# A hybrid decoder step on one core: old-state products split, residuals fused, z projected during GLA

## The chip, the cores and the metric

The kernel runs on one core of a Trainium2 chip. The metric is the time on the device, in microseconds. Engines are TensorE (PE, its weight loads PEld), VectorE (DVE), ScalarE (ACT), GpSimd (POOL) and SyncE (SP), which issues the transfers.

## The reference, cut to what matters

One layer: RMSNorm, a parallel mixer of gated DeltaNet (8 heads of 128) and GLA (4 heads, 128 by 256), a merge, then a mixture of 32 experts. There are 304 tokens: 272 of a prompt, taken in chunks, and 8 sequences of 4 tokens that begin from given old states.

```
p = h @ w_in                      # q, k, v | z | b, a | q_b, k_b, v_b, r_b | lr | g_a, g_b
# gated DeltaNet, a chunk: M = I + beta * (k k^T) * decay, strictly lower
value, kcd = solve(M, [beta*v, beta*exp(G)*k])
v_new = value - kcd @ S
o_a   = (q*exp(G)) @ S + (q k^T * decay) @ v_new
S     = S*exp(GL) + (k*exp(GL-G))^T @ v_new
# GLA, a chunk: o_b = (q*exp(B)) @ S + A @ v ;  S = S*exp(BL) + (k*exp(BL-B))^T @ v
o_a = rmsnorm(o_a, norm_a) * silu(z)
o_b = rmsnorm(o_b, norm_b) * silu(r_b)
merged = sigmoid(g_a) * (o_a @ w_proj_a) + sigmoid(g_b) * (o_b @ w_proj_b)
x = x + merged @ w_out ;  x = x + experts(rmsnorm(x)) ;  y = rmsnorm(x)
```

## The kernel before

Five functions run one behind the other with a barrier between them: `front` (qkv projection, convolution, norms), `delta` (DeltaNet), `gla`, `merge` (the other projections, gates, output projection), `experts`. Each has one hand-written program per engine; an engine works in the order written, and semaphores are the only links.

**Weights.** A load `n` brings 1 MB (256 columns of `w_in`, or a quarter of a projection) into one of eight ring slots (`load_w`, L223; the slot from `slot(n)`, L69) as soon as PE has used the slot's last content (`unit_done`). ACT makes a rounded high part (`high_part`, L246), DVE or POOL the low part (`low_part`, L252), and PE multiplies a block of 128 columns as 24 matmuls of 304 columns, three for each of 8 slices (`block_of_slot`, L261): two blocks to a load. Loads 20 to 23 are z (N_Z is 20), 24 to 27 are r, 28 to 35 the gates, 36 to 43 the two projections, 44 to 47 `w_out`. Blocks of merge are counted from z: 0 to 7 are z, 8 to 15 r, 16 to 31 the gates, 32 to 47 the projections.

**delta.** PE first does the tail's products (the last 48 tokens: 16 of the prompt, 32 of the samples), then eight q and k projections for GLA with the tail's solve between them (L1202 to L1248), then `old_products` of both halves (L1194, 64 instructions for each 4 heads: the old states, 128 by 128, times 8 columns of keys and queries), then two chunks of 128 tokens. A chunk works on two halves of four heads, `hh`, with a solve whose three last rounds (`for r in range(3)`, L1318) alternate between PE, DVE and ACT; then residual, new values, output and state (L1338 to L1360). In chunk 1 the residual is two DVE operations on 512 columns (L1132, L1133), the state update two more (L1140, L1141), and the same holds for the tail (L1153, L1154, L1173, L1174). POOL prepares gates, masked keys (L975) and decays the old states (L924). DVE copies the old-state products out in 16 pieces (L1092), and POOL's gates of the second half wait for both halves of them (L935).

**gla.** After gate products (L1617, L1618) and decays (L1625, L1627), twelve steps `i`, one per chunk and head: `exps(i + 2)`, ACT's exponents, POOL's scaled keys (L1468), DVE's scaled queries (L1585), `pairs` (L1653), mask and sum on DVE (L1597, L1598), output and state. The last four heads carry the sample states, loaded by SP at the start of the stage (L1442).

**merge.** Twelve norms with blocks 0 to 3 in between (L1867 to L1879), then blocks 4 to 47 (L1880); a block's PSUM bank is free when the block four before it has been read, for z and r by ACT's silu (L1793). DVE gates with it (L1832), ACT and POOL split the gated heads into high and low parts (L1798, L1772). Then comes `w_out`, and the experts start on the result.

## Time and profile before

| | |
|---|---|
| median of 3 runs | 1051.42 us (1048.2 to 1053.07) |
| the profiled execution | 1056.28 us, span 1054.6, mean granted clock 0.873 |
| PE busy in the span | 916.8 us, 87% |
| DVE, ACT, POOL busy | 400.2, 294.3, 282.2 us |
| transfers | 175.67 MB, mean 167 GB/s |

The stages, by the first PE instruction of each: delta from 183.8 us, gla from 410.3, merge from 531.7, the expert stage from about 752. A granted clock of 1.00 is 2.4 GHz and 0.50 is 1.2 GHz. An operation's line is its place in the kernel before; a helper's line (L250, L256, L270 to L272) stands for all its callers. A row of a timeline is start, length, engine, line, operation and, in brackets, the idle time before it and what ended it.

### The profile page before, as it was taken

The numbers are of one execution on the slowest core, as the hardware profiler recorded it, in microseconds if no ns is written. First come the engines' busy times: TensorE is split into PE (matmuls) and PEld (weight loads), VectorE is DVE, ScalarE is ACT, GpSimd is POOL, SyncE is SP. The second block draws the span as 40 slices with busy tenths as digits, with TensorE's granted clock in tenths as the row PEclk, the third lists the DMA queues.
The fourth block names the chain that finished last, engine by engine and source line by source line (L and its number), as shares of the span: only waits on it lengthen the run. The fifth ranks groups of instructions, "written<-read, shape, count | busy, mean of one in ns | idle before, by whom it ended". The sixth has DMA issues, their size and how long they took to land. (4 is left out here: it accounts for less than half of the span.)

```text
span 1054.6 us, 15090 instructions
## 1 busy us (share of the span) xinstructions
PE 916.8 (87%) x6318; PEld 752.7 (71%) x6318; DVE 400.2 (38%) x701; ACT 294.3 (28%) x579; POOL 282.2 (27%) x209
## 2 busy tenths in 40 slices
PE   4989989999989698669988999999669998998963
PEld 3989978998989695446568999999556444444521
DVE  4367833302445432352456531662340222210213
ACT  5453466211222213220056443331201111110102
POOL 7544323313675211133154103755000000000000
PEclk8889999896999755798878999999856999999996
DMA  9624400230000026301485544410471999999981
GB/s 266 202 83 153 153 13 13 83 80 1 2 1 1 1 80 215 125 1 60 140 245 169 160 160 159 160 41 1 170 329 61 421 420 420 420 420 419 419 352 48
DMA packets 97908, 175.67 MB, mean 167 GB/s; under 512 B 8965, under 2 KB 84325, under 8 KB 85494
## 3 DMA queue, kind: packets, MB, share of 16 engines
q1 hardware_dynamic: 97832, 174.62, 45.9%
q8 instruction: 54, 0.88, 0.4%
q14 instruction: 22, 0.17, 0.1%
HBM read 163.66 MB, written 10.95 MB: 166 GB/s over the span
## 5 line engine op out<-in xcount | busy, mean ns | idle before, releaser
L270 PE MATMUL ps<-rounded,rounded 128*128 128x304 f32 x640 | 202.7, 317 | 7.6 <-POOL rounded L256 3.5
L272 PE MATMUL ps<-rounded,rounded 128*128 128x304 f32 x640 | 198.5, 310 | 0.0
L271 PE MATMUL ps<-hL,rounded 128*128 128x304 f32 x512 | 160.4, 313 | 0.0
L256 POOL TENSOR_TENSOR rounded<-ring,rounded 128x2048 fp32r<-128x2048 f32 x24 | 111.1, 4630 | 179.7 <-ACT rounded L250 173.9
L270 PEld LDWEIGHTS ps<-rounded,rounded 128*128 128x128 f32 x640 | 126.1, 197 | 9.4 <-POOL rounded L256 3.7
L272 PEld LDWEIGHTS ps<-rounded,rounded 128*128 128x128 f32 x640 | 125.9, 197 | 0.0
L271 PEld LDWEIGHTS ps<-hL,rounded 128*128 128x128 f32 x512 | 102.1, 199 | 0.4 <-issue 0.2
L250 ACT ACTIVATE rounded<-ring 128x2048 fp32r<-128x2048 f32 x47 | 89.6, 1911 | 27.1 <-PE ps L272 16.0
L2172 DVE TENSOR_TENSOR arena<-arena,ps 128x512 f32<-128x512 f32 (+1 forms) x48 | 32.9, 685 | 123.2 <-PE ps L2290 123.2
L2220 PE MATMUL ps<-arena 128*128 128x128 f32 (+1 forms) x384 | 74.7, 328 | 2.5 <-DVE arena L2139 2.5
L2220 PEld LDWEIGHTS ps<-arena 128*128 128x128 f32 (+1 forms) x384 | 57.1, 204 | 21.6 <-issue 6.2
L2237 PE MATMUL ps<-ring,arena 128*32 128x256 f32 x1024 | 63.2, 404 | 10.2 <-DMA ring<-in_expert_w_up 10.2
L256 DVE TENSOR_TENSOR rounded<-ring,rounded 128x2048 fp32r<-128x2048 f32 x24 | 56.2, 2341 | 36.2 <-ACT rounded L250 36.0
L2237 PEld LDWEIGHTS ps<-ring,arena 128*32 128x32 f32 x1024 | 35.6, 116 | 34.4 <-issue 17.5
L1259 PE MATMUL ps<-arena 128*128 128x128 f32 x448 | 57.1, 288 | 1.1 <-DVE arena L1106 1.1
L1259 PEld LDWEIGHTS ps<-arena 128*128 128x128 f32 x448 | 55.0, 202 | 2.3 <-DVE arena L1106 1.6
L2290 PE MATMUL ps<-arena 128*128 128x512 f32 (+1 forms) x96 | 45.7, 610 | 6.5 <-ACT arena L2062 6.5
L2290 PEld LDWEIGHTS ps<-arena 128*128 128x128 f32 (+1 forms) x96 | 12.9, 166 | 39.5 <-DVE arena L2172 22.0
L2277 PE MATMUL ps<-arena 128*32 128x512 f32 x256 | 31.9, 642 | 9.1 <-DMA arena<-in_expert_w_down 5.0
L2040 ACT ACTIVATE arena<-ps 128x512 f32<-128x512 f32 x16 | 9.6, 597 | 108.5 <-PE ps L2220 108.5
L271 PE MATMUL ps<-rounded,rounded 128*128 128x304 f32 x128 | 38.6, 301 | 0.0
L676 DVE SCALAR_TENSOR_TENSOR arena<-ps,small,arena 128x271 f32<-128x271 f32 (+2 forms) x72 | 35.9, 499 | 2.5
(383 smaller groups left out, 1542.1 us busy)
## 6 DMA issues: line engine op xcount, KB each, us to landing
ring<-in_w_in SPq DMA_DIRECT2D x36, 1024.0 KB, 7.0
ring<-in_expert_w_gate SPq DMA_DIRECT2D x32, 1024.0 KB, 14.4
ring<-in_expert_w_up SPq DMA_DIRECT2D x32, 1024.0 KB, 19.4
arena<-in_expert_w_down SPq DMA_DIRECT2D x32, 1024.0 KB, 17.8
arena<-in_state_gla SPq DMA_DIRECT2D x4, 1024.0 KB, 5.5
out_sg_s<-arena SPq DMA_DIRECT2D x4, 1024.0 KB, 4.1
ring<-in_w_proj_a SPq DMA_DIRECT2D x4, 1024.0 KB, 5.2
ring<-in_w_proj_b SPq DMA_DIRECT2D x4, 1024.0 KB, 5.1
```

Source lines behind the costliest of these rows:

```text
L250: self.nc.scalar.activation(HI[n % 3], self.ring[:, slot(n), :], ACT.Copy).then_inc(self.w_hi, 1)
L256: on.tensor_tensor(self.LOW[:, slot(n), :], self.ring[:, slot(n), :], HI[n % 3], ALU.subtract).then_inc(self.w_lo, 1)
L270: self.nc.tensor.matmul(self.psum[b][:, 0:NT], h[:, j, c], xh(j), start=(j == 0), stop=False)
L271: self.nc.tensor.matmul(self.psum[b][:, 0:NT], h[:, j, c], xl(j), start=False, stop=False)
L272: ins = self.nc.tensor.matmul(self.psum[b][:, 0:NT], lo[:, j, c], xh(j), start=False, stop=(j == KB - 1))
L676: ins = nc.vector.scalar_tensor_tensor(o[:, r:], x[:, 0:TP - r], cw[:, 3 - r, b:b + 1], o[:, r:], ALU.mult, ALU.add)
L1259: ins = mm(bank4(b)[:, h, :], lhs[:, h, :], rhs[:, h, :], start=True, stop=True)
L2172: V.tensor_tensor(y, y, psum[6 + x % 2][0:L[c], :], ALU.add).then_inc(s["y_added"], 1)
L2220: ins = mm(bank4(6 + h)[:, j, :], XN[0:l, c, 128 * b:128 * b + 128], P[0:l, c, :], start=(c == 0), stop=(c == 2))
L2237: ins = mm(psum[kind][32 * i:32 * i + 32, 0:256], XG[:, j, 32 * i:32 * i + 32], w[:, j, :], start=(j == 0), stop=(j == KB - 1))
L2277: ins = mm(psum[4 + half][32 * i:32 * i + 32, :], HX[:, j, 32 * i:32 * i + 32], w[:, j, 512 * half:512 * half + 512], start=(j == 0), stop ...
L2290: mm(psum[6 + x % 2][0:L[c], :], PT[:, T0[c]:T0[c] + L[c]], OG[:, 512 * half:512 * half + 512], start=True, stop=True).then_inc(s["sc_done ...
```

## The change

1. **delta, order.** The first projection block stands ahead of the tail's products; each later one moves up by one place. ACT's evacuations follow.
2. **delta, old-state products.** The first half stays ahead of chunk 0. The second half, into bank 0, stands between rounds 1 and 2 of chunk 0, on keys that POOL has copied aside (`KQ1`). DVE copies each half in two pieces instead of eight; POOL's gates wait for the first half alone.
3. **delta, residuals.** Multiplication and addition are one `scalar_tensor_tensor` for each head, in chunk 1's residual and state and in the tail's.
4. **z in gla.** Loads 20 and 21 go to slots 2 and 3 during delta, 22 and 23 to slots 0 and 1 at the start of gla. The eight z blocks stand in gla: 0 behind the gate products, 1 ahead of `exps(0)`, 2 behind it, 3 to 7 in steps 0 to 4. ACT copies them into `ZR`. Two high parts lie where the sample states go, so those are loaded after the last z block. `exps` of the first two chunks share banks 0 and 1, since the blocks take 4 and 5.
5. **merge.** Blocks 8 to 11 (r) stand between the norms, and PE goes on with 12; the silus of z read `ZR` and wait for no block. Loads of the final norm and the router wait for the eighth gating. The remaining buffers are laid out anew.

```diff
-    return (n if n < N_Z else n + 4) % SLOTS
+    return (n + 6) % 8 % 4 if N_Z <= n < N_Z + 4 else n % SLOTS
...
-        if n >= 3:
-            act.wait_ge(self.unit_done, units(n - 2))
...
+        for n in range(N_Z, N_Z + 2):
+            k.load_w(sp, n)
...
+        V_.tensor_copy(KQ1[:, :, :, :], KQ[:, 4:8, :, TAIL:]).then_inc(s["keys_copied"], 1)
...
-                pl.wait_ge(s["ksq_done"], 2)
-                pl.wait_ge(s["keys_copied"], 2)
+                pl.wait_ge(s["ksq_done"], 1)
+                pl.wait_ge(s["keys_copied"], 3)
...
+        block_out(0)
...
-        block_out(0)
+        block_out(1)
...
+        def old_products_kept(hh, b):
+
+            dve.wait_ge(s["ksq_done"], hh + 1)
+            dve.wait_ge(s["keys_copied"], 3)
+            both = psum[b][:, 0:256].rearrange("p (h b n r) -> p h b n r", h=4, b=8, n=2)
+            for n, dst in enumerate((KT, oaT)):
+                ins = nc.vector.tensor_copy(dst[:, 4 * hh:4 * hh + 4, T0[2] + TAIL:NT].rearrange("p h (b r) -> p h b r", r=TS), both[:, :, :, n, :])
+            ins.then_inc(s["ksq_ready"], 1)
+        old_products_kept(0, 4)
...
+                if c == 0 and r == 1:
+                    old_products_kept(1, 0)
...
                     dve.wait_ge(s["ks_done"], hh + 1)
-                    link(nc.vector.tensor_tensor(w[bB], bank4(b0), bc_last(nbeg[:, c, hs], 128), ALU.mult))
-                    nc.vector.tensor_tensor(w[bB], w[bB], V[:, c, hs, :], ALU.add).then_inc(s["r_ready"], 1)
+                    for h in range(4):
+                        ins = nc.vector.scalar_tensor_tensor(w[bB][:, h, :], bank4(b0)[:, h, :], nbeg[:, c, 4 * hh + h:4 * hh + h + 1], V[:, c, 4 * hh + h, :],
+                                                             ALU.mult, ALU.add)
+                    ins.then_inc(s["r_ready"], 1)
                 dve.wait_ge(s["vn_done"], i + 1)
...
-            link(nc.vector.tensor_tensor(S[:, hs, :], S[:, hs, :], bc_last(egl3[:, 0, hs], 128), ALU.mult))
-            nc.vector.tensor_tensor(S[:, hs, :], S[:, hs, :], bank4(4 * hh + 2), ALU.add).then_inc(s["s_ready"], 1)
+            for h in range(4):
+                ins = nc.vector.scalar_tensor_tensor(S[:, 4 * hh + h, :], S[:, 4 * hh + h, :], egl3[:, 0, 4 * hh + h:4 * hh + h + 1], bank4(4 * hh + 2)[:, h, :],
+                                                     ALU.mult, ALU.add)
+            ins.then_inc(s["s_ready"], 1)
...
-                             KQ[:, h, :, TAIL + TS * b:TAIL + TS * b + TS], start=True, stop=True)
+                    t = slice(TAIL + TS * b, TAIL + TS * b + TS) if hh == 0 else slice(TS * b, TS * b + TS)
+                    ins = mm(psum[bank][:, 64 * h + 8 * b:64 * h + 8 * b + 8].rearrange("p (n r) -> p n r", n=2), sample_state(4 * hh + h)[:, b, :],
+                             (KQ if hh == 0 else KQ1)[:, h, :, t], start=True, stop=True)
             ins.then_inc(s["ksq_done"], 1)
+        projection(0)
...
-        projection(0)
+        projection(1)
...
-        old_products(0)
-        old_products(1)
+        old_products(0, 4)
...
+                if c == 0 and r == 1:
+                    pe.wait_ge(s["keys_copied"], 3)
+                    old_products(1, 0)
...
-    TL = [k.carve(2432 + 512 * p, 512) for p in range(2)]
...
+    TL = [k.carve(18816 + 512 * p, 512) for p in range(2)]
+    HI = [k.carve_r(14720 + SW * p, SW) for p in range(2)]
+    ZR = k.carve(2432, 8 * NT, 8, NT)
...
+        for n in range(N_Z + 2, N_Z + 4):
+            k.load_w(sp, n)
+        sp.wait_ge(unit_done, units(N_Z + 4))
...
-        for n in range(N_Z, N_Z + 4):
+        for n in range(N_Z + 4, N_Z + 8):
             k.load_w(sp, n)
...
+        def block_out(b):
+            act.wait_ge(unit_done, first_block + b + 1)
+            nc.scalar.activation(ZR[:, b, :], psum[b if b < 2 else 4 + b % 2][:, 0:NT], ACT.Copy).then_inc(s["zr_ready"], 1)
+        k.high_part(act, N_Z, HI)
...
+            if c == 0:
+                k.high_part(act, N_Z + 1, HI)
+        block_out(0)
...
+        block_out(1)
+        k.high_part(act, N_Z + 2, HI)
...
-                a, b = bank4(4 * p), bank4(4 * p + 1)
+                a, b = bank4(0 if c < 2 else 4 * p), bank4(1)
...
+                if 1 <= i < 7:
+                    block_out(i + 1)
+                    if i == 2:
+                        k.high_part(act, N_Z + 3, HI)
...
+        k.low_part(dve, nc.vector, N_Z, HI)
...
+        k.low_part(dve, nc.vector, N_Z + 1, HI)
...
+            if i in (0, 2):
+                k.low_part(dve, nc.vector, N_Z + 2 + i // 2, HI)
...
+        def projection(b):
+            if b >= 4:
+                pe.wait_ge(s["zr_ready"], b - 1)
+            k.block_of_slot(pe, N_Z + b // 2, b % 2, b if b < 2 else 4 + b % 2, HI)
+        projection(0)
...
             if c < 2:
-                mm(psum[4 * p][:, :], lg, GR[:, 0:4, :], start=True, stop=True)
-                mm(bank4(4 * p + 1)[:, 0, :], lg, GR[:, 4, :], start=True, stop=True).then_inc(s["ex_done"], 1)
+                if i == 1:
+                    pe.wait_ge(s["ex_ready"], 1)
+                mm(psum[0][:, :], lg, GR[:, 0:4, :], start=True, stop=True)
+                mm(bank4(1)[:, 0, :], lg, GR[:, 4, :], start=True, stop=True).then_inc(s["ex_done"], 1)
...
+        projection(1)
+        pe.wait_ge(s["zr_ready"], 2)
         exps(0)
+        projection(2)
         exps(1)
         pairs(0)
         for i in range(SC3):
@@ -1666,7 +1724,11 @@
             if i + 2 < SC3:
                 if c == 2 and h >= 2:
                     pe.wait_ge(s["su_ready"], 8 * (h - 1))
+                if i == 7:
+                    pe.wait_ge(s["zr_ready"], 8)
                 exps(i + 2)
+            if i < 5:
+                projection(i + 3)
...
+        for n in range(N_Z + 8, N_Z + 12):
+            k.load_w(sp, n)
...
+        sp.wait_ge(s["gated"], 8)
...
-        for n in range(N_Z + 4, N_PRE):
+        for n in range(N_Z + 12, N_PRE):
             k.load_w(sp, n)
...
-        for n in range(N_Z, N_Z + 3):
+        for n in range(N_Z + 4, N_Z + 7):
             k.high_part(act, n, HI)
...
         for u in range(16):
-            act.wait_ge(unit_done, base + u + 1)
+            if u >= 8:
+                act.wait_ge(unit_done, base + u + 1)
             if u >= 2:
                 act.wait_ge(s["gated"], u - 1)
-            nc.scalar.activation(ZT[:, u % 2, :], psum[u % 4][:, 0:NT], ACT.Silu).then_inc(s["silu_ready"], 1)
-            if u % 2:
+            nc.scalar.activation(ZT[:, u % 2, :], ZR[:, u, :] if u < 8 else psum[u % 4][:, 0:NT], ACT.Silu).then_inc(s["silu_ready"], 1)
+            if u % 2 and u >= 8:
                 k.high_part(act, N_Z + u // 2 + 3, HI)
...
             if h in (3, 5, 7, 9):
-                u = (h - 3) // 2
-                k.block_of_slot(pe, N_Z + u // 2, u % 2, u, HI)
-        for u in range(4, 48):
+                u = 8 + (h - 3) // 2
+                k.block_of_slot(pe, N_Z + u // 2, u % 2, u % 4, HI)
+        for u in range(12, 48):
```

## Rows read from the trace of the kernel before

**Rows 1.** The page's slices of 26.4 us: granted clock of PE in tenths
```profile
PEclk8889999896999755798878999999856999999996
```
**Rows 2.** The chain that ended last, its first piece: start, length, what
```profile
751.91 4.31 DMA arena<-in_norm_ffn
```
**Rows 3.** Windows: stretch, length, busy PE PEld DVE ACT POOL, clock, DMA share, GB/s
```profile
568.00:594.80 26.80, 26.80 (x195) 26.80 (x194) 16.28 (x14) 12.34 (x17) 11.00 (x6) 1.00 0.47 135
...
870.00:1040.00 170.00, 145.47 (x1170) 74.10 (x1169) 33.47 (x66) 19.56 (x39) 0.00 (x0) 0.96 0.92 380
```
**Rows 4.** Windows, the same columns, start of delta
```profile
184.00:192.00 8.00, 7.35 (x64) 6.86 (x63) 1.22 (x3) 2.36 (x3) 5.92 (x10) 0.60 0.74 212
192.00:197.00 5.00, 5.00 (x24) 4.91 (x25) 3.42 (x4) 0.54 (x2) 3.87 (x3) 0.62 0.30 91
```
**Rows 5.** Windows and PE's timeline, the old-state products
```profile
228.00:233.50 5.50, 5.50 (x51) 5.50 (x49) 0.00 (x0) 0.42 (x1) 3.04 (x3) 0.98 0.00 0
...
237.20:250.80 13.60, 13.60 (x65) 13.60 (x65) 0.00 (x0) 0.00 (x0) 0.00 (x0) 0.50 0.00 1
...
228.31 9.08 PE L1199 MATMUL ps<-arena 128*128 128x8 f32 x64
237.23 13.80 PE L1199 MATMUL ps<-arena,ring 128*128 128x8 f32 x64
```
**Rows 6.** Timelines of DVE, POOL and PE, the residual in chunk 1
```profile
342.45 0.69 DVE L1132 TENSOR_TENSOR arena<-ps,small 128x512 f32<-128x512 f32 x1 [0.20 <-PE ps L1343]
343.17 3.97 DVE L1133 TENSOR_TENSOR arena<-arena 128x512 f32<-128x512 f32 x1
...
340.55 4.18 POOL L975 TENSOR_TENSOR arena<-arena,seg 48x1152 f32<-48x1152 f32 x2 [4.16 <-PE ps L1259]
...
347.20 2.08 PE L1347 MATMUL ps<-arena 128*128 128x128 f32 x8 [4.79 <-DVE arena L1133]
```
**Rows 7.** Windows, behind that residual
```profile
347.20:358.40 11.20, 8.85 (x41) 8.36 (x41) 3.37 (x5) 0.60 (x1) 1.71 (x1) 0.60 0.01 1
```
**Rows 8.** Short DVE operations: a timeline row, and a group by line
```profile
178.50 1.64 DVE L708 TENSOR_SCALAR arena<-ps,small 128x128 f32<-128x128 f32 x6 [1.76 <-PE ps L717]
...
L1573 DVE SCALAR_TENSOR_TENSOR arena<-arena,ps 128x256 f32<-128x256 f32 x32 | 13.9, 477 | 4.3 <-PE ps L1701 4.3
```
**Rows 9.** Windows, two steps of gla and its last heads
```profile
439.66:446.93 7.27, 5.67 (x19) 4.20 (x19) 2.88 (x4) 1.24 (x4) 1.90 (x1) 0.64 0.00 0
446.93:452.19 5.26, 3.09 (x19) 2.24 (x19) 2.91 (x4) 1.21 (x4) 1.90 (x1) 1.00 0.00 0
...
479.45:528.85 49.40, 48.15 (x190) 29.25 (x190) 16.84 (x43) 3.46 (x15) 11.59 (x10) 0.84 0.32 107
```
**Rows 10.** PE's timeline, gla before the steps
```profile
423.72 1.12 PE L1625 MATMUL ps<-masks,ring 128*128 128x128 f32 x4 [2.72 <-DVE arena L1551]
...
431.45 1.13 PE L1635 MATMUL ps<-masks,arena 128*128 128x512 f32 x2 [1.47 <-DVE arena L1556]
```
**Rows 11.** PE's timeline, pair products of two steps of gla
```profile
439.66 2.08 PE L1653 MATMUL ps<-arena 128*128 128x128 f32 x8 [2.64 <-DVE arena L1585]
...
452.19 1.13 PE L1653 MATMUL ps<-arena 128*128 128x128 f32 x8 [2.17 <-POOL arena L1468]
```
**Rows 12.** ACT's timeline and a window, merge behind the norms
```profile
561.30 0.74 ACT L1793 ACTIVATE arena<-ps 128x304 f32<-128x304 f32 x2
...
561.77:568.00 6.23, 6.23 (x25) 6.23 (x26) 4.99 (x5) 5.64 (x8) 3.74 (x3) 0.51 0.27 85
```
**Rows 13.** The gatings (L1832), and timelines of DVE, POOL and ACT in merge
```profile
L1832 DVE TENSOR_TENSOR oaT<-oaT,arena x8: 465/791/1120, 561.8 to 578.6; 128x304 f32<-128x304 f32 x8
...
573.73 2.29 DVE L256 TENSOR_TENSOR rounded<-ring,rounded 128x2048 fp32r<-128x2048 f32 x1 [1.24 <-ACT rounded L250]
574.12 2.61 POOL L1772 TENSOR_TENSOR rounded<-oaT,rounded 128x304 fp32r<-128x304 f32 x1 [2.34 <-ACT rounded L1798]
...
571.79 1.91 ACT L250 ACTIVATE rounded<-ring 128x2048 fp32r<-128x2048 f32 x1
```

More of the change, by code:

```diff
@@ L247, in high_part @@
         self.arrived(act, n)
-        if n >= 3:
-            act.wait_ge(self.unit_done, units(n - 2))
-        self.nc.scalar.activation(HI[n % 3], self.ring[:, slot(n), :], ACT.Copy).then_inc(self.w_hi, 1)
+        if n >= len(HI):
+            act.wait_ge(self.unit_done, units(n - len(HI) + 1))
+        self.nc.scalar.activation(HI[n % len(HI)], self.ring[:, slot(n), :], ACT.Copy).then_inc(self.w_hi, 1)
     def low_part(self, eng, on, n, HI):
@@ L867, in delta @@
     KQ0 = k.shaped(k.ring[:, 6, 1760:2016], (8, 2, TAIL))
+    KQ1 = k.shaped(k.ring[:, 7, 1760:2016], (4, 2, NB * TS))
     s = named(nc, "delta", """xg_ready sb_ready diff_done kk_done eg_done dt_ready eg_ready b_ready at1_ready at_ready qe_ready
@@ L1012, in _ @@
             nc.scalar.activation(tD8[hh][0:l3], four48(psum, 2 * hh, 0)[0:l3], ACT.Copy).then_inc(s["tail_d8"], 1)
-        for b in range(4, 8):
+        for b in range(5, 8):
             block_out(b)
@@ L1086, in _ @@
                 nc.vector.tensor_tensor(y, y, four48(psum, 2 * hh + 1, off)[0:l3], ALU.add).then_inc(ready, 1)
-        dve.wait_ge(s["ksq_done"], 2)
-        both = psum[4][:, :].rearrange("p (h b n r) -> p h b n r", h=8, b=8, n=2)
-        dve.wait_ge(s["keys_copied"], 2)
-        for n, dst in enumerate((KT, oaT)):
-            for h in range(8):
-                ins = nc.vector.tensor_copy(dst[:, h, T0[2] + TAIL:NT].rearrange("p (b r) -> p b r", r=TS), both[:, h, :, n, :])
-        ins.then_inc(s["ksq_ready"], 1)
+        def old_products_kept(hh, b):
[6 more added lines that the diff above has]
+        old_products_kept(0, 4)
         for c in range(2):
@@ L1152, in _ @@
             r = w[bY][0:l3, :, :]
-            link(nc.vector.tensor_tensor(r, bank4(4 * hh + 1)[0:l3], bc_last(nbeg[0:l3, 2, hs], 128), ALU.mult))
-            nc.vector.tensor_tensor(r, r, V[0:l3, 2, hs, :], ALU.add).then_inc(s["r_ready"], 1)
+            for h in range(4):
+                ins = nc.vector.scalar_tensor_tensor(r[:, h, :], bank4(4 * hh + 1)[0:l3, h, :], nbeg[0:l3, 2, 4 * hh + h:4 * hh + h + 1], V[0:l3, 2, 4 * hh + h, :],
+                                                     ALU.mult, ALU.add)
+            ins.then_inc(s["r_ready"], 1)
         for hh in range(2):
@@ L1172, in _ @@
             dve.wait_ge(s["ds_done"], 4 + hh + 1)
-            link(nc.vector.tensor_tensor(S[:, hs, :], S[:, hs, :], bc_last(egl3[:, 0, hs], 128), ALU.mult))
-            nc.vector.tensor_tensor(S[:, hs, :], S[:, hs, :], bank4(4 * hh + 2), ALU.add).then_inc(s["s_ready"], 1)
+            for h in range(4):
+                ins = nc.vector.scalar_tensor_tensor(S[:, 4 * hh + h, :], S[:, 4 * hh + h, :], egl3[:, 0, 4 * hh + h:4 * hh + h + 1], bank4(4 * hh + 2)[:, h, :],
+                                                     ALU.mult, ALU.add)
+            ins.then_inc(s["s_ready"], 1)
     @block.tensor
@@ L1220, in _ @@
             ins.then_inc(s["tail_dT"], 1)
-        projection(1)
+        projection(2)
         for hh in range(2):
@@ L1226, in _ @@
             four48_of(2 * hh + 1, 0, tD[hh], tB[hh]).then_inc(s["tail_sq"], 1)
-        projection(2)
+        projection(3)
         for hh in range(2):
@@ L1234, in _ @@
             four48_of(2 * hh, 192, tD2[hh], tB2[hh]).then_inc(s["tail_p4"], 1)
-        projection(3)
+        projection(4)
         for hh in range(2):
@@ L1240, in _ @@
             four48_of(2 * hh, 0, tB4[hh], tD4[hh]).then_inc(s["tail_p8"], 1)
-        projection(4)
+        projection(5)
         for hh in range(2):
@@ L1245, in _ @@
             four48_of(2 * hh + 1, 192, tD8[hh], tY[:, 4 * hh:4 * hh + 4, :]).then_inc(s["tail_p9"], 1)
-        projection(5)
         projection(6)
@@ L1656, in pairs @@
             ins.then_inc(s["pair_done"], 1)
+        projection(1)
+        pe.wait_ge(s["zr_ready"], 2)
         exps(0)
+        projection(2)
         exps(1)
@@ L1817, in _ @@
     def _(dve):
-        for n in range(N_Z, N_Z + 3):
+        for n in range(N_Z + 4, N_Z + 7):
             k.low_part(dve, nc.vector, n, HI)
@@ L1832, in _ @@
             nc.vector.tensor_tensor(v, v, ZT[:, u % 2, :], ALU.mult).then_inc(s["gated"], 1)
-            if u % 2:
+            if u % 2 and u >= 8:
                 k.low_part(dve, nc.vector, N_Z + u // 2 + 3, HI)
@@ L1902, in _ @@
             pe.wait_ge(k.w_lo, n + 1)
-            hi, lo = (w.rearrange("p (j c) -> p j c", j=KB) for w in (HI[n % 3], k.LOW[:, slot(n), :]))
+            hi, lo = (w.rearrange("p (j c) -> p j c", j=KB) for w in (HI[n % len(HI)], k.LOW[:, slot(n), :]))
             if u >= 4:
```

45 lines of the change are left out of this document (24 added, 21 removed).

## Prediction

> **What bounds the kernel now.** I read the slices of the page first, then the chain that ended last, then the windows of each stage, then the timelines where TensorE waits. The profiled execution takes 1056.28 us (span 1054.6 and 1.7 around it); the median of the runs is 1051.42, 4.9 below. I make the sum against 1056.3 and carry it to the median unchanged. The chain [rows 2] reaches back only to 751.9 us, to a load that starts the expert stage. From 870 us that stage is bound by transfers [rows 3]; they start only when the ring is free, so it moves as a whole with the end of merge, and a microsecond saved or lost before 752 counts in full. Before 752 every stage is a train led by TensorE: in merge it is dense at full clock [rows 3], in delta and gla it waits for other engines and drops to the lower of its two levels (1.2 of 2.4 GHz) several times [rows 1].
>
> The price of one projection block of 24 matmuls: 568.0 to 594.8 holds eight (blocks 5 to 12) with PE busy throughout at clock 1.00, so 26.8/8 = **3.35 us**; block 4, from 561.77, took 6.23 at clock 0.51 [rows 3, 12].
>
> **A. First projection ahead of the tail's products (delta).** Nothing is added. Between 184 and 192 PE runs the tail's small products at clock 0.60, and the first projection after them takes to 197 at 0.62 [rows 4]: 5 us instead of 3.35, and the tails would take some 4.6 instead of 8. If the dense block in front keeps the clock up, 1.7 + 3.6 = 5.3 us are gained. But PE stands still at the barrier just before, in both kernels, so the drop may come in the moved block; then up to 1 us is lost, and the level falls also where small products have run a while [rows 5]. I take **2 saved** (range -1 to 5). Between the tail's steps there is one block each as before, with two instead of three behind the last; its result is wanted only after the first old-state products.
>
> **B. Second half of the old-state products.** Today 64 instructions take from 228.3 to 237.2 and 64 more from 237.2 to 250.8, the second lot wholly at clock 0.50 [rows 5]. The change starts the first chunk behind the first lot: everything after moves up 13.6 us. Gate products on POOL, then needed after one lot only, move with it, and the DVE's two (formerly 16) copies are 0.5 us beside PE's first products. The second lot then stands between round 1 and round 2, where PE has hardly a gap (40 instructions of 0.11 us fill a round), so it is on the path. Its price: nearest is the first lot, which came in at full clock and fell to 0.50 about 5 us later: 8.9 us. Until the level is back another 1.5 (3 us of dense work at half speed, about what block 4 lost [rows 12]). Saved 13.6 - 8.9 - 1.5 = **3** (bounds: 6.6 if the clock holds, 64 at 5.5/51 = 0.108; 0 or a little below if it falls at once and 13.6 is paid again). The DVE copies behind it (two of 128 columns, about 0.6 us) lie under PE's 1.1 us of round 2's first products.
>
> **C. Fused residuals.** In chunk 1 the residual of the first half is two DVE operations: 0.69 from PSUM, then an addition of two SBUF tiles that took 3.97 instead of 0.69 while POOL ran its masked keys; PE stood 4.79 us and then worked at clock 0.60 until 358.4 [rows 6, 7]. The fused form is four operations of 128 columns with one source in PSUM. Six back-to-back 128-column operations took 1.64, and one of this kind with 256 columns takes 0.478, so one is about 0.35 and each further 0.26: 0.35 + 3 x 0.26 = 1.13 us [rows 8]. The DVE operation with a PSUM source at 342.45 ran its plain 0.69 beside the busy POOL, so I take no stall. First half: 4.69 - 1.13 = 3.56. The other pairs cost 1.42 today, 1.13 after: the state update and the second residual stand one behind the other before PE (0.55), the last update and the tail residual 0.55 more. With a gap of 1.3 instead of 4.79 the clock should hold; the work from 347.2 to 358.4 at full clock saves 4.1 (some 40 instructions at 0.11 instead of 0.21, the two speeds in [rows 5]). Together **8.5** (low end 3.5: the clock drops all the same and the four operations pipeline worse; high end 9).
>
> The Trainium skill (SBUF — State Buffer, Who interferes with whom) says that a VectorE instruction with two SBUF inputs and a GpSimd one that reads SBUF exclude each other for a whole instruction, and that one with at most one SBUF input does not. The rows agree (3.97 against 0.69), and nothing in the sum hangs on the page.
>
> **D. z projection between the steps of gla.** Added: eight blocks on PE, eight evacuations (0.4 each, as the silus of [rows 12]) and four high parts (1.91) on ACT, four low parts (2.29) on DVE [rows 13]. Most of ACT's and DVE's part has cover: their busy share of a step is under 3 of 5.3 us [rows 9]. Step by step on PE:
> - Start. The gate products keep PE to 421; then it waited for DVE to 423.7 [rows 10]. Block 0 takes 421.0 to about 425.5 and raises the clock; the decays behind it run faster and end at 431, as before. Cost 0.
> - Block 1 and its evacuation stand ahead of the first exponents, which start at 431.1 + 3.35 + 0.6 = 435.1 instead of 431.45. Block 2 runs between exponents 0 and 1 to 439.8, over their ACT and POOL work; exponents 1 (1.1), ACT (0.9) and DVE (mask, sum and queries, 2.5 of the 2.9 us of its four operations) follow, and the second pair products start at 444.9. They started at 439.66, after DVE too [rows 11]. Cost 5.2.
> - Steps 0 to 4 carry a block each. Today a full-clock step is 5.26 us with PE busy 3.09, and PE waits 2.17 for POOL [rows 9, 11]. ACT's 1.2 and POOL's 1.90 for the next but one now run under the block, so the step becomes PE's own, 3.09 + 3.35 less the 0.15 that its last result drains = 6.3, and 6.7 in the fifth, which has the state products. Today the five take 439.66 to 468.88, 29.2 (two of them slowed by the clock, one 7.27), after that 4 x 6.3 + 6.7 = 31.9. Cost 2.7.
> - The two steps behind and the last four heads are as before; their loads wait for the last block (about 475) and need 5.5 us, wanted at 487.
> Cost of D: **8** (5 if dense work spares the later drops too, the last heads running at 0.84 today [rows 9]; 13 if low parts meet POOL's products twice and the clock still falls).
>
> **E. Merge.** Eight of 44 blocks go: 26.8. But the silus and gatings of z stay, and block 12 must wait for the silu of block 8, that is for nine silus in a row, now with PE standing. The first silu starts at 561.3, right behind the last norm [rows 12]. Per head ACT has a silu (0.37) and a copy of the same size, 0.75 us. DVE's gating and POOL's low part use SBUF sources only and shut each other out: at 574.1 POOL's operation took 2.61 beside DVE's 2.29, and gatings took 0.47 to 1.12, so POOL's own part is 1.12 - 0.47 = 0.65 [rows 13]. In turns that is 1.12 per head. ACT's order alone makes the eight heads 6 us, the turns make them 9; I take 8.4, near the turns, since the first two gatings find POOL idle. By the Trainium skill's exclusive port pair (same page and section) the two would alternate just so, which gives the 9. PE starts block 12 at 561.7 + 8.4 = 570, at low clock as block 4 did, and ends it at 576.3, against 594.8 today. Saved **18.4** (15.5 to 20.5). Behind it all is PE-bound as now: high part 27 is ready about 3 us before block 14 wants it; loads 32 on wait for the eighth gating but are wanted 40 us later.
>
> **Sum:** 2 + 3 + 8.5 - 8 + 18.4 = 24 saved. 1056.3 - 24 = 1032.3 for a profiled execution, 1051.4 - 24 = **1027.5** for the median.
>
> **Rivals.**
> 1. *The blocks hide in gla entirely and the gates cost only ACT's time* (D 3, E 20.5, B 6, C 9, A 4): 36 saved, 1015. For it: PE idles 2.2 us in each step. Against: a block is 3.35. Chance 0.1.
> 2. *The clock eats the gains.* If the drops stay in delta (A -1, B 0, C 3.5), the steps of gla cost 13, the gates 15.5: 5 to 10 saved, 1041 to 1046. For it: small products pull the level down [rows 5]. Chance 0.15.
> 3. *Slower: gla at the low level.* Should the clock stay at 1.2 GHz through the steps, as it does in the page's slices 15 and 16 (369 to 422) [rows 1], PE's own step is 12.6 instead of 6.3, five times 31 more, and blocks 0 to 2 cost 3 x 2.9 more: D becomes 48, against 18.4 from merge and the 2.5 that delta keeps in rival 2: 27 slower, 1078. It decides from D above 21, that is from low clock in a third of this work. Against: dense blocks of this kind raised the clock each time [rows 3, 12]. Chance 0.02.
> 4. *The fused form doesn't escape POOL* (C 0.5, the stall stays): 16 saved, 1035.5. Chance 0.08; the forecast as summed, 1021 to 1036 as its own range, 0.65.
>
> **How the numbers follow.** The forecast is 1027.5. Taking the bounds of A to E together, not all at one end, gives 1018 to 1040; reaching to the better part of rivals 1 and 2: 1015 to 1043. About 0.5% (5 us) is what a measurement of this kernel can tell from no change. Faster by more: the forecast, rivals 1 and 4, most of 2: 0.93; within: 0.04; slower: 0.03.
>
> **What would show it.** A: no half-clock stretch in the first 8 us of delta. B: L1199's first lot ahead of the chunk, the second between the rounds taking 7 to 9 us. C: r_ready about 1.2 us behind L1343 and clock 1.0 after. D: PE idle by exponents 0, steps of 6.3 us, gla 8 us longer. E: a hole in PE of about 11 us before block 12, merge 18 us shorter, the expert stage as long as before. The prediction is wrong if the hole is nearer 16 us, if a step of gla is above 7 us, or if the expert stage changes its length.

## The result, and the profile after

| | before | after |
|---|---|---|
| median of 4 runs each | 1052.24 us (1048.2 to 1054.33) | 1036.96 us (1036.4 to 1039.51) |
| ratio, 95% interval | | 0.986 (0.983 to 0.990) |
| span of the profiled execution | 1054.6 us | 1034.6 us |
| mean granted clock | 0.873 | 0.885 |
| PE busy | 916.8 us | 904.1 us |

The change saves 15.3 us by the medians and 20.0 by the two spans; 24 were forecast, and the time of 1027.5 was 9.5 too low. Both spans were cut at the same marks: the first PE instruction of delta, of the old-state products, of chunk 0, of gla, of the first exponents and of merge, and the load at which the chain [rows 2] begins. In microseconds:

| stretch | before | after | saved |
|---|---|---|---|
| up to delta | 183.87 | 184.19 | -0.3 |
| delta, up to the old-state products (A) | 44.44 | 40.93 | 3.5 |
| old-state products ahead of chunk 0 (B) | 22.58 | 8.67 | 13.9 |
| the chunks and the tail (B and C) | 159.38 | 161.71 | -2.3 |
| gla, up to the first exponents (D) | 21.18 | 28.08 | -6.9 |
| gla, the rest (D) | 100.30 | 107.81 | -7.5 |
| merge (E) | 220.16 | 200.06 | 20.1 |
| experts | 302.69 | 303.15 | -0.5 |

The slices of the granted clock, in tenths, and the first piece of the chain, as in [rows 1, 2]:

```profile
PEclk8889999999899855999768899999757999999996
...
731.45 4.64 DMA arena<-in_norm_ffn
```

The tenth slice no longer falls to 6, where the second lot of old-state products stood; the 8 behind it is that lot in its new place. The 8, 5 and 5 from the fourteenth on are the fall in delta's tail and in gla's gate products, there as before.

Windows of delta after (columns as in [rows 3]). The first three are the first projection, the tail's products and the second projection (answering [rows 4]); the next two the first lot of old-state products, then the second lot in two pieces and what follows it ([rows 5]); the last two lie behind the first residual of chunk 1 ([rows 7]).

```profile
184.19:187.69 3.50, 3.50 (x24) 3.33 (x24) 0.00 (x0) 1.92 (x1) 3.50 (x6) 1.00 0.44 120
187.69:192.40 4.71, 4.71 (x66) 4.38 (x65) 1.22 (x3) 0.96 (x3) 2.20 (x5) 1.00 0.98 282
192.40:197.47 5.07, 5.07 (x25) 4.89 (x25) 3.43 (x4) 0.54 (x2) 4.45 (x5) 0.66 0.28 82
225.12:229.00 3.88, 3.88 (x38) 3.88 (x36) 0.00 (x0) 0.42 (x1) 3.05 (x3) 1.00 0.61 164
229.00:233.79 4.79, 4.79 (x30) 4.79 (x30) 0.00 (x0) 0.00 (x0) 0.00 (x0) 0.65 0.25 86
270.05:275.00 4.95, 4.95 (x47) 4.95 (x45) 0.69 (x1) 0.00 (x0) 3.38 (x2) 0.98 0.01 3
275.00:279.25 4.25, 4.25 (x22) 4.25 (x22) 0.00 (x0) 0.00 (x0) 0.00 (x0) 0.50 0.00 0
279.25:281.95 2.70, 2.70 (x14) 2.70 (x14) 0.49 (x2) 0.00 (x0) 0.00 (x0) 0.50 0.00 0
...
339.70:343.50 3.80, 3.80 (x22) 3.80 (x21) 0.00 (x0) 0.60 (x1) 2.33 (x2) 0.56 0.02 4
343.50:354.78 11.28, 8.15 (x66) 7.08 (x65) 5.76 (x22) 4.79 (x16) 0.00 (x0) 1.00 0.00 0
```

The second lot, from 270.05 to 279.25, takes 9.2 us: both lots now start at full clock and end at half. The residual of chunk 1, from the timelines of DVE, POOL and PE (start, length, engine, line, operation; line numbers are those of the kernel after, L1143 answers L1132 and L1133 in [rows 6]):

```profile
336.01 1.13 DVE L1143 SCALAR_TENSOR_TENSOR arena<-ps,small,arena 128x128 f32<-128x128 f32 x4 [0.20 <-PE ps L1365]
...
334.11 4.18 POOL L979 TENSOR_TENSOR arena<-arena,seg 48x1152 f32<-48x1152 f32 x2 [4.16 <-PE ps L1277]
...
337.19 1.16 PE L1369 MATMUL ps<-arena 128*128 128x128 f32 x8 [1.22 <-DVE arena L1143]
...
354.78 2.16 PE L1399 MATMUL ps<-arena,ring 48*48 48x128 f32 x16 [0.58 <-DVE arena L1168]
```

POOL's masked keys lie over the fused residual as they lay over the addition before, and DVE isn't held up: PE stands 1.22 us. The last row is the tail's solution products, which still find full clock.

In gla, two windows behind the gate products and rows from the timelines of ACT and PE up to the first exponents (L1690), then rows of PE and DVE at the seam of two steps (L1754 the state product, L1611 DVE's copy of it, L1708 the pair products, answering [rows 11]):

```profile
411.90:416.40 4.50, 4.32 (x20) 1.91 (x18) 1.38 (x2) 1.62 (x3) 0.00 (x0) 1.00 0.00 0
416.40:423.10 6.70, 5.20 (x25) 4.89 (x24) 0.68 (x1) 0.59 (x1) 0.00 (x0) 0.75 0.00 0
...
423.11 0.42 ACT L1525 ACTIVATE arena<-ps 128x304 f32<-128x304 f32 x1 [6.01 <-PE ps L272]
...
423.58 1.13 PE L1690 MATMUL ps<-masks,arena 128*128 128x512 f32 x2 [0.51 <-ACT arena L1525]
...
445.81 0.60 PE L1754 MATMUL ps<-ring,arena 128*128 128x256 f32 x2
447.02 1.13 PE L1708 MATMUL ps<-arena 128*128 128x128 f32 x8 [0.61 <-DVE arena L1611]
...
446.45 0.42 DVE L1611 COPY arena<-ps 128x256 f32<-128x256 f32 x1 [2.44 <-PE ps L1754]
```

The decays end at 416.4. The window behind them holds one z block and lasts 6.7 us; PE is busy in 5.2 of them. In a step the last thing PE does is the state product, and the next pair products wait for DVE's copy of it.

In merge, windows of the hole and of block 12, then rows of ACT, DVE, POOL and PE (L1861 the silus, L1900 the gatings, L1839 POOL's low parts), answering [rows 12, 13]:

```profile
559.02:569.06 10.04, 0.00 (x0) 0.00 (x1) 8.61 (x12) 8.54 (x20) 6.09 (x7) 0.62 0.00 0
569.06:575.30 6.24, 6.24 (x25) 6.24 (x26) 5.66 (x7) 5.00 (x6) 1.88 (x2) 0.51 0.70 153
...
560.07 1.28 ACT L1861 ACT_TABLE_LOAD   x1
561.37 0.80 ACT L1861 ACTIVATE arena<-arena 128x304 f32<-128x304 f32 x2
...
563.27 5.95 DVE L1900 TENSOR_TENSOR oaT<-oaT,arena 128x304 f32<-128x304 f32 x6 [0.48 <-ACT arena L1861]
...
562.97 7.97 POOL L1839 TENSOR_TENSOR rounded<-oaT,rounded 128x304 fp32r<-128x304 f32 x8 [7.70 <-ACT rounded L1866]
...
569.06 0.62 PE L270 MATMUL ps<-rounded,rounded 128*128 128x304 f32 x1 [10.04 <-ACT arena L1861]
...
L1900 DVE TENSOR_TENSOR oaT<-oaT,arena x8: 468/1094/1097, 561.9 to 568.1; 128x304 f32<-128x304 f32 x8
```

The last row has the least, median and greatest time of z's gatings, in ns. DVE and POOL run side by side at one operation each per 1.0 us, and PE waits 10.04 us (the hole, as it is called below), then needs 6.2 us for a block at half clock.

### The profile page after: what moved, and what is told of

Read it like the earlier page. It is cut to its first block and busy times, and to the rows that moved or that the text cites. A ratio compares the mean times of both kernels' runs of the same rounds, so it can differ in the third digit from the quotient of the medians.

```text
span 1034.6 us, 15097 instructions
## 1 busy us (share of the span) xinstructions
PE 904.1 (87%) x6318; PEld 742.8 (72%) x6318; DVE 398.5 (39%) x705; ACT 297.5 (29%) x587; POOL 275.8 (27%) x210
## 5 line engine op out<-in xcount | busy, mean ns | idle before, releaser
L271 PE MATMUL ps<-hL,rounded 128*128 128x304 f32 x512 | 162.9, 318 | 0.0
L270 PEld LDWEIGHTS ps<-rounded,rounded 128*128 128x128 f32 x640 | 127.9, 200 | 22.8 <-ACT arena L1861 10.5
L272 PEld LDWEIGHTS ps<-rounded,rounded 128*128 128x128 f32 x640 | 127.9, 200 | 0.0
L271 PEld LDWEIGHTS ps<-hL,rounded 128*128 128x128 f32 x512 | 104.2, 203 | 0.4 <-issue 0.2
L2358 PEld LDWEIGHTS ps<-arena 128*128 128x128 f32 (+1 forms) x96 | 12.9, 166 | 39.6 <-DVE arena L2240 22.0
```

The lines of the kernel that those rows point to most:

```text
L270: self.nc.tensor.matmul(self.psum[b][:, 0:NT], h[:, j, c], xh(j), start=(j == 0), stop=False)
L271: self.nc.tensor.matmul(self.psum[b][:, 0:NT], h[:, j, c], xl(j), start=False, stop=False)
L272: ins = self.nc.tensor.matmul(self.psum[b][:, 0:NT], lo[:, j, c], xh(j), start=False, stop=(j == KB - 1))
L2358: mm(psum[6 + x % 2][0:L[c], :], PT[:, T0[c]:T0[c] + L[c]], OG[:, 512 * half:512 * half + 512], start=True, stop=True).then_inc(s["sc_done ...
```

## The experiments

Each ratio is against runs of the kernel before on the same chip; differences of medians between two edited kernels can be between two chips. Every edit starts from the changed kernel, but for the first run and for "A, B and C alone", which start from the kernel before.

**The kernel before once more.** No edit.

> The kernel before, unchanged, profiled a second time. The sum was made against a profiled execution of 1056.28 us (span 1054.6), 4 us above the median of its runs. If that execution carried a disturbance of its own in one stage, this one comes out near 1050 to 1052 and one stage is some 4 us shorter than in the first trace; if a profiled execution of this kernel is longer as such, it comes out near 1056 again with the same stage marks (delta from 183.8, gla from 410.3, merge from 531.7, experts from 751.9).

Measured: median 1053.69 us (ratio 1.001, 0.998 to 1.003), span 1051.9. Every stretch of the table agrees with the first trace within 0.15 us but two: 184.54 up to delta, and 156.24 instead of 159.38 in chunks and tail. The same 136 products of chunk 0's solve, in a window of the first trace and one of this:

```profile
263.08:280.21 17.13, 17.13 (x136) 16.99 (x137) 6.06 (x9) 5.73 (x10) 11.05 (x8) 0.90 0.01 1
```
```profile
263.70:279.30 15.60, 15.54 (x137) 15.40 (x138) 6.11 (x10) 5.75 (x10) 11.11 (x8) 1.00 0.01 2
```

The first execution has a dip of the clock (a short fall to the lower level) in both chunks, the second in neither. So part of the profiled execution's surplus over the median is chance of the clock, 1.6 us a chunk, and comparing two spans carries an error of 3 us or more. That can be most of what stands between 20.0 and 15.3.

**A undone.**

```diff
-        projection(0)
         for hh in range(2):
...
-        projection(1)
+        projection(0)
...
-        projection(5)
...
+        projection(5)
         projection(6)
```

> The changed kernel with its projections back behind the tail's products (and ACT's evacuations with them), nothing else. Theory (the dense block in front keeps the clock up through the tail's small products): from delta's first product to the first old-state product it takes 44.4 us instead of 40.9, with a stretch at half clock between 2 and 8 us into the stage; 3.5 us slower than the changed kernel. Rival (where the clock falls there is chance, the order of the products matters little): under 1.5 us slower, and the half-clock stretch is as long as in the changed kernel.

Measured: 1042.13 us, ratio 0.991 (0.987 to 0.994). From delta's first product to the old-state products 44.47 us (181.90 to 226.37) instead of 40.93, every later stretch up to the experts within 0.1 us of the changed kernel's. Window of the tail's products:

```profile
184.00:192.00 8.00, 8.00 (x48) 7.64 (x49) 2.74 (x7) 1.08 (x4) 5.04 (x9) 0.50 0.90 260
```
```profile
183.44 0.56 PE L1228 MATMUL ps<-masks,arena 48*48 48x48 f32 x8 [0.65 <-POOL arena L908]
```

The theory holds in the stretch: 3.5 us. The tail's products run at 0.50 here and at 1.00 behind the block. Not all of it is the clock: here PE also stands 0.65 us for POOL in the tail's products, and behind the block it doesn't. The medians say 5.2, but the two intervals of the ratio overlap, so the times alone would not show the part.

**B undone.**

```diff
         old_products(0, 4)
+        pe.wait_ge(s["keys_copied"], 3)
+        old_products(1, 0)
...
-                if c == 0 and r == 1:
-                    pe.wait_ge(s["keys_copied"], 3)
-                    old_products(1, 0)
```

> The changed kernel with both lots of old-state products ahead of chunk 0 again (banks, copied keys and POOL's waits stay as changed). Theory (a lot costs 9.3 us in fresh clock, 13.6 behind another one): the second lot takes 13.6 us at half clock, chunk 0 begins 13.6 us later, and its rounds lose the 9.2 of the lot and 2.7 of half-clock work behind it; net 2 to 3 us slower than the changed kernel. Rival (64 such instructions cost the same wherever they stand, the forecast's 8.9 was luck): within 1 us of the changed kernel.

Measured: 1040.86 us, ratio 0.989 (0.985 to 0.992). PE's timeline:

```profile
226.63 8.88 PE L1217 MATMUL ps<-arena 128*128 128x8 f32 x64
235.37 13.80 PE L1217 MATMUL ps<-ring 128*128 128x8 f32 x64
249.84 2.05 PE L1293 MATMUL ps<-arena 128*128 128x128 f32 x8 [0.67 <-DVE oaT L1099]
```

Chunk 0 starts 14.5 us later (0.67 of it a wait for copies that this edit adds), chunks and tail take 150.60 instead of 161.71: 3.4 us net, and 2.8 without the added wait. The theory's 2 to 3 us hold; 64 such instructions cost 13.8 us directly behind 64 others and 9.2 between the rounds.

**C undone.**

```diff
-                    for h in range(4):
-                        ins = nc.vector.scalar_tensor_tensor(w[bB][:, h, :], bank4(b0)[:, h, :], nbeg[:, c, 4 * hh + h:4 * hh + h + 1], V[:, c, 4 * hh + h, :],
-                                                             ALU.mult, ALU.add)
-                    ins.then_inc(s["r_ready"], 1)
+                    link(nc.vector.tensor_tensor(w[bB], bank4(b0), bc_last(nbeg[:, c, hs], 128), ALU.mult))
+                    nc.vector.tensor_tensor(w[bB], w[bB], V[:, c, hs, :], ALU.add).then_inc(s["r_ready"], 1)
```

The state updates and the tail's residual and update go back the same way.

> The changed kernel with the residuals and state updates of delta as two operations each again. Theory (the addition of two SBUF tiles is shut out by POOL, the fused form with one source in PSUM is not): in chunk 1 the addition takes 3.3 to 4.0 us beside POOL's masked keys, PE stands 4.1 to 4.8 us instead of 1.22 and works at half clock behind it; 8 us slower than the changed kernel. Rival (the fused form is shorter, but what took the 4 us away is that POOL's masked keys stand elsewhere since the old-state products moved): the addition takes 0.7, PE stands 1.6 us, and it is 1.5 to 2.5 us slower.

Measured: 1044.34 us, ratio 0.993 (0.989 to 0.996). DVE, POOL and PE in chunk 1:

```profile
337.53 0.69 DVE L1142 TENSOR_TENSOR arena<-ps,small 128x512 f32<-128x512 f32 x1 [0.21 <-PE ps L1357]
338.26 3.97 DVE L1143 TENSOR_TENSOR arena<-arena 128x512 f32<-128x512 f32 x1
...
335.63 4.17 POOL L979 TENSOR_TENSOR arena<-arena,seg 48x1152 f32<-48x1152 f32 x2 [4.16 <-PE ps L1269]
...
342.28 2.07 PE L1361 MATMUL ps<-arena 128*128 128x128 f32 x8 [4.79 <-DVE arena L1143]
```

The addition takes 3.97 us again and PE stands 4.79: the rival falls. (POOL goes on behind its masked keys with the decay of the old states, so it stays busy to the addition's end.) Chunks and tail are 8.2 us longer. The two stretches of gla together give back 0.6 and merge 0.7, since the clock falls elsewhere; 6.9 remain, and the medians say 7.4. One of these places matters further on, gla's second z block and the exponents behind it:

```profile
427.06 0.41 PE L270 MATMUL ps<-rounded,rounded 128*128 128x304 f32 x1 [1.47 <-DVE arena L1593]
...
431.18 1.12 PE L1682 MATMUL ps<-masks,arena 128*128 128x512 f32 x2 [0.51 <-ACT arena L1517]
```

PE stands the same 1.47 us ahead of the block, but the block runs at full clock, and the stretch up to the exponents is 25.82 us instead of 28.08.

**A, B and C alone**, on the kernel before: its delta stage replaced by the changed one, without the early z loads.

> The kernel before with the delta stage of the changed kernel (parts A, B and C) and nothing of z's move (D, E). Theory (the parts add as the traces' stage marks say: A 3.5, B 3.2, C 8.3 saved, D 14.4 lost, E 19.1 saved): 15 us faster than before, about 1037.5, and the stages behind delta as in the kernel before (gla 121.5 us, merge to block 12 63 us). Rival (gain in delta is partly given back in gla by where the clock falls): gla 2 to 4 us longer than 121.5, 1040 to 1042, so that z's move is worth 4 us or more.

Measured: 1040.93 us, ratio 0.986 (0.982 to 0.991). Delta is as in the changed kernel (40.93, 8.78, 161.71), gla 122.6 us instead of 121.5, merge 220.49. The stretches of delta are the theory's; gla gives back 1.1 us, where the theory said none and the rival 2 to 4; the time is in the rival's range (1040 to 1042), 3.4 us above the theory's. The move of z adds 6.4 us to this by the stretches, 4.0 by the medians (on different chips), and nothing by the ratios (0.986 both, each good to about 4 us): that it is worth something as built is likely from the traces and not shown by the times.

**The z block behind the state product.**

```diff
-            if i < 5:
-                projection(i + 3)
             if i >= 2:
                 pe.wait_ge(s["oT_ready"], i - 1)
...
                VB[0:l, h, c, :], start=True, stop=True).then_inc(s["ds_done"], 1)
+            if i < 5:
+                projection(i + 3)
```

> The changed kernel, but in steps 0 to 4 of gla the z block stands behind the state product instead of ahead of the output products. Theory (the copy behind the block): a step is 7.05 us, of which PE is busy 6.44, and 0.61 is the wait for DVE's copy of the state product, which nothing covers because that product is the last thing in PE's order; with the block behind it the copy lies under 3.4 us of PE, the step becomes 6.45 and five of them save 3.0 us. Rival (DVE or ACT too full: evacuation, high and low parts): the wait moves to another releaser, POOL's keys or DVE's queries, the step stays near 7.0, and nothing is saved (within 1 us).

Measured: 1027.95 us, ratio 0.979 (0.972 to 0.985). PE's timeline, one step:

```profile
443.75 1.05 PE L1708 MATMUL ps<-arena 128*128 128x128 f32 x8
...
446.17 0.60 PE L1752 MATMUL ps<-ring,arena 128*128 128x256 f32 x2
449.94 1.05 PE L1708 MATMUL ps<-arena 128*128 128x128 f32 x8
```

No wait is left in the step, and it is 6.19 us instead of 7.05: the 0.61 of the wait and another 0.25, for without a stop one instruction starts before the last one has ended. The five steps take 31.5 instead of 35.8; gla behind the first exponents takes 103.08 instead of 107.81. That is 4.7 us; the medians are 9.0 apart, but the four times of this run spread from 1023.4 to 1037.0, and its trace has 1.7 us less in merge, which the edit doesn't touch.

**The second z block ahead of the wait.**

```diff
+        pe.wait_ge(s["kdec_ready"], 2)
+        projection(1)
         pe.wait_ge(s["kd_ready"], 3)
         pe.wait_ge(s["kdec_ready"], 3)
...
-        projection(1)
-        pe.wait_ge(s["zr_ready"], 2)
+        pe.wait_ge(s["zr_ready"], 1)
         exps(0)
```

> The changed kernel, but the second z block stands directly behind the decays, into a bank of its own, ahead of the wait for DVE's last decay product, and the first exponents follow it without a wait for its evacuation; the third high part stands behind the first exponents' reading on ACT. Theory (a block behind a wait): today PE is idle 1.5 us behind the decays, then works 1.8 us longer than at full clock, and stands 0.5 for the evacuation; the first exponents come 3.6 us after the decays' end instead of 7.1, so 3.5 to 4 us are saved up to the steps, which keep their length. Rival (what is late is DVE and ACT, not PE): the exponents come earlier but the first pair products do not, and less than 1.5 us is saved.

Measured: 1030.99 us, ratio 0.980 (0.978 to 0.982). The stretch up to the first exponents is 24.06 us instead of 28.08, the rest of gla 107.72. These 4.0 us are the stop of 1.5 us, the half clock behind it and the wait for the evacuation, and all three are gone: the block follows the decays without a stop and runs at full clock. The medians are 6.0 apart; in this trace delta's chunks and tail, which the edit doesn't touch, are 3.0 us shorter as well.

```profile
413.73 1.05 PE L1681 MATMUL ps<-arena,masks 48*48 48x512 f32 x2
418.16 1.02 PE L1691 MATMUL ps<-masks,arena 128*128 128x512 f32 x2
```

**POOL's low parts behind the ninth gating.**

```diff
+        pl.wait_ge(s["gated"], 9)
         for j in range(8):
             pl.wait_ge(s["oah_ready"], j + 1)
```

> The changed kernel, but POOL's low parts of the gated heads wait for the ninth gating; ACT's copies stay between the silus. Theory (turns: POOL's subtraction and DVE's gating, both on SBUF sources alone, shut each other out): the gatings of z take 0.47 each instead of 0.99, the period of a head falls from 1.02 to what ACT needs, 0.74 to 0.80, and the hole before block 12 from 10.0 us to 8.0 to 8.9. Rival (ACT's chain with its wait for the gating sets the period): gatings stay near 1.0, or fall without the period falling, and the hole stays within 0.3 of 10.0.

A gating of z takes 0.48 us instead of 1.09, a head 0.69 instead of 1.02 (a little under the theory's 0.74), and the hole is 8.39 us. The period is then ACT's own, silu and copy. There is a single execution, of 1030.96 us; it serves for the rows alone, since such times differ by more than the 1.65 us in question.

```profile
562.28 0.48 DVE L1901 TENSOR_TENSOR oaT<-oaT,arena 128x304 f32<-128x304 f32 x1 [0.22 <-ACT arena L1862]
...
565.03 0.62 PE L270 MATMUL ps<-rounded,rounded 128*128 128x304 f32 x1 [8.39 <-ACT arena L1862]
```

**ACT's copies, and with them POOL's low parts, between the later sigmoids.**

```diff
-            if 1 <= u <= 8:
-                act.wait_ge(s["gated"], u)
-                nc.scalar.activation(OAH[u - 1], oaT[:, u - 1, :], ACT.Copy).then_inc(s["oah_ready"], 1)
...
+            if u < 24:
+                act.wait_ge(s["gated"], 16)
+                nc.scalar.activation(OAH[u - 16], oaT[:, u - 16, :], ACT.Copy).then_inc(s["oah_ready"], 1)
```

> The changed kernel, but ACT's copies of the gated heads, and with them POOL's low parts, stand between the later sigmoids; the order of the silus and the banks stay. Theory (turns): a head costs one gating of 0.47 and little more, about 0.5 instead of 1.02, so the silu of block 8 comes 4 us earlier and the hole is 6 to 6.7 us. Rival (the silu waits for the gating two back, with a semaphore's way each time): 0.8 a head, hole 8 us or more.

```profile
561.42 3.85 DVE L1900 TENSOR_TENSOR oaT<-oaT,arena 128x304 f32<-128x304 f32 x8 [0.85 <-ACT arena L1861]
...
565.46 0.62 PE L270 MATMUL ps<-rounded,rounded 128*128 128x304 f32 x1 [6.95 <-ACT arena L1861]
```

Again a single execution, of 1031.60 us: 0.50 a head and a hole of 6.95, 0.25 above the theory's end. Taken away in this order, the turns of DVE and POOL made 1.65 of the 10.04 us and ACT's copies 1.44; what is left, 6.95, is the table load, eight heads at the pace of DVE and the silu of block 8.

**Merge without the hole.**

```diff
+    GATED = [8, 9, 10, 11, 0, 1, 2, 3, 4, 5, 6, 7, 12, 13, 14, 15]
+    def bank(u):
+        return 4 + u % 4 if 12 <= u < 16 else u % 4
...
-        for u in range(16):
+        k.high_part(act, N_Z + 7, HI)
+        for t, u in enumerate(GATED):
...
-            if u - 4 < 16:
-                pe.wait_ge(s["silu_ready"], u - 3)
+            if u < 16:
+                pe.wait_ge(s["rs_ready"], u - 3)
+            elif u < 20:
+                pe.wait_ge(s["silu_ready"], GATED.index(u - 8) + 1)
```

> The changed kernel, but in merge the blocks 12 to 15 go to the four banks that the norms have left, load 27's high part stands ahead of the silus, the silus and gatings of r come before those of z, and the high copies of the gated heads move between the later sigmoids. Theory (the hole is a matter of banks and order only): PE goes on from the norms at 559 without a stop; the hole of 10.0 us and the 2.9 us that block 12 loses at half clock are both gone, 12.9 us saved, about 1024 us. Rival (the work is only put off): ACT and DVE are late for blocks 14 to 19 instead (the high and low parts of loads 27 and 28 or the silus), PE stands there for 5 us or more and under 8 us are saved.

Measured: 1024.30 us, ratio 0.974 (0.971 to 0.977), merge 187.62 us instead of 200.06. A window from the norms on, and the gatings (as in the last row above):

```profile
560.20:605.00 44.80, 44.80 (x324) 44.80 (x323) 26.18 (x27) 29.81 (x44) 13.69 (x8) 1.00 0.66 203
```
```profile
L1907 DVE TENSOR_TENSOR oaT<-oaT,arena x8: 468/470/476, 570.0 to 573.4; 128x304 f32<-128x304 f32 x8
```

In this window PE never stops and keeps the full clock: 12.4 us saved of the theory's 12.9. Behind it PE stands for DVE as in the changed kernel (1.2 and 2.4 us at its two longest waits), so the work isn't only put off.

**The three together.**

> The three rearrangements together: z blocks behind the state products in the steps of gla, the second z block directly behind the decays in a bank of its own, and merge without the hole. By the traces they saved, against the changed kernel's, 4.3 us in the five steps, 3.7 ahead of the first exponents, and 12.9 in merge: 21 us, about 1016. Theory (they stand in different stages and add up): 1014 to 1018. Rival (PE, less delayed, now finds a load or a weight part late, or the clock falls elsewhere): 1019 to 1024.

Measured: **1014.67 us**, ratio 0.964 (0.960 to 0.967): 22.3 us under the changed kernel and 37.9 under the one before, 21.3 by the stretches (4.05 up to the exponents, 4.8 in the rest of gla, 12.4 in merge). By the stretches they add up (4.0, 4.7 and 12.4 alone). The single medians promise more, 27.6, and the clock's chance in them doesn't add. This version beats both kernels.

## Why the prediction was right or wrong, step by step

**What bounds the kernel**: right. The expert stage moved as a whole and kept its length, 303.15 us instead of 302.69.

**A**: 3.5 for a forecast of 2. The step was a value between two ends. With the block in front the tail runs in 4.71 us at clock 1.00, but the drop comes after it: the second projection takes 5.07 instead of 3.35. 5.3 less 1.7 is about what was found; undoing A gives the same. The sum put all of it down to the clock, and 0.65 of it is a wait for POOL that the block covers.

**B**: 3.2 for 3, and each term: 13.9 ahead of the chunk (13.6), 9.2 for the lot (8.9). Behind it the half clock costs 2.7 (1.5 assumed), which a dip less in chunk 0's solve, 1.6, hides in this trace. So the part itself is worth 13.9 - 9.2 - 2.7 = 2.0, and that the trace has 3.2 is luck; the run with B undone gives 3.4, or 2.8 without the wait that its edit adds.

**C**: 8.3 for 8.5. The fused residual takes 1.13 as worked out, beside a busy POOL. One term was wrong in kind: the clock does not hold behind it. It falls from 339.7 to 343.5 (0.56), 3.8 us instead of 11.2; that loses 1.8 of the 4.1, and the tail's solution products, which now begin at full clock (2.16 us for 16 instead of 3.64), give it back. By the Trainium skill (SBUF — State Buffer, Who interferes with whom), a VectorE instruction with at most one SBUF input, outside the modes that use two ports, doesn't contend with GpSimd; the 1.13 and the 3.97 of the run without the fused form agree.

**D**: the step that failed, 14.4 for 8, and outside its bound of 13. Two terms:
- *The start*, 6.9 for 3.7. The sum let block 1 follow the decays. In the order it stands behind a wait for DVE's last decay product: PE stands 1.5 us, then needs 5.2 for the block instead of 3.35, since the clock is at half for most of it, then 0.51 for the evacuation. The wait was in the rows, 1.47 us ahead of the first exponents [rows 10]; the sum took its end, 431, for the end of the decays. The run with the block ahead of the wait took all of this back. The fall of the clock is no sure consequence of the stop: with C undone the same stop came without it.
- *The steps*, 6.55 for 2.7: 7.05 us each instead of 6.3. The sum added PE's own 3.09 and 3.35 and asked only whether POOL and ACT find cover. It forgot who waits for the last instruction in PE's order: the pair products two steps on share the bank of the state product and wait for DVE's copy of it. Before, that copy lay under the 2.17 us that PE waited for POOL anyway [rows 11]; with POOL hidden it is the next thing late, 0.61 and a drain of 0.25. The run with the block behind the product shows both gone (6.19).

The first exponents to the second pair products came out as worked out (9.3 for 9.8). By the prediction's own test (a step above 7 us) this is wrong, if only by 0.05.

**E**: 20.1 for 18.4; 19.1 up to the end of block 12, another 1.0 behind it, where the kernel before has one more dip (0.83 from 715 to 725 us; the one after has none from 700 on). The hole was forecast at about 11 and is 10.04, with a head at 1.02 (1.12 assumed), and block 12 takes the 6.2 at half clock. The turns of DVE and POOL are shown: 1.09 beside POOL, 0.47 without.

**The rivals.** *Hidden entirely*: D is 14.4, not 3. *The clock eats the gains*: its drops in delta came, but shorter or later (3.8 us instead of 11.2 behind the residual), and of the 6.4 us that D cost over the forecast the clock made 1.8. A, C and E kept their gains. *Slower at low clock*: the steps ran at 1.00 throughout. *The fused form doesn't escape POOL*: its figure of 16 saved matches the medians (15.3) by accident; the mechanism is refuted by 1.13 against 3.97.

**The sum.** The median came 9.5 us above the forecast, in two about equal parts. Against its own execution: 1032.3 forecast, 1036.4 measured, and the 4 us are D (-6.4) less what A and E did better (+1.5 and +1.7), and the stretches that nothing was forecast for (-0.8). Carrying it unchanged to the median was the second error, about 5 us: the profiled execution before lay 4 to 5 us above its median, partly by dips of the clock that the one after had fewer of, while the one after lay at the foot of its runs.

## What to carry to other kernels

When work fills an engine's wait, look for what else was hidden in that wait: list who waits for the last instruction of the step and for its bank, and put the filler behind that instruction, not ahead of it. And filler that needs nothing from a wait belongs ahead of it in the order: behind it, the stop costs its own length and, in most traces here, clock on top. A chain of small work that holds up a dense engine can be only a matter of order and of banks: here free banks and the needed results first took away 12.4 us, a hole and a slow block, without removing any work.

## What the runs showed of the hardware

The same program falls to the lower clock at different places in different executions: chunk 0's 136 products took 17.13 us (clock 0.90) in one execution of the kernel before and 15.54 in another, while every stretch without such a dip agreed within 0.15 us. It can be more: in the run with ACT's copies late, whose gla is the changed kernel's, gla behind the first exponents took 113.00 us instead of 107.81, and with POOL's low parts late the fall in delta's second projection did not come (39.43 us up to the old-state products instead of 40.93).

A short stop ahead of dense work can cost more than its length. The 1.5 us in which PE stood before gla's second z block were followed by a block of 5.2 us (window at 0.75) instead of 3.4; so it was in seven of the eight traces that have this stop, and in the eighth, with C undone, the block ran at full clock. In the two traces without the stop it ran at full clock too. The 10 us of standing in merge cost the next block 2.9. The block without the stop, from the run with the second z block ahead of the wait:

```profile
415.00:418.10 3.10, 3.10 (x24) 3.10 (x24) 0.68 (x1) 0.42 (x1) 0.00 (x0) 1.00 0.00 0
```
